# The sums of squares of the pre-norms by four column groups of 32, in a two-layer hybrid decoder step

## The reference

```
def rms_norm(x, g):
    xf = x.astype(F32)
    y = xf * lax.rsqrt(jnp.mean(xf * xf, axis=-1, keepdims=True) + RMS_EPS)
    return (y * g.astype(F32)).astype(x.dtype)
...
mod = (jax.nn.silu(c) @ a_w + a_b).reshape(B, N_SUB, 3, D_MODEL)[:, :, :, None, :]
def modulate(y, i):
    return rms_norm(y, g_pre[i]) * (1.0 + mod[:, i, 1]) + mod[:, i, 0]
def residual(y, out, i, w):
    return y + w * mod[:, i, 2] * rms_norm(out, g_post[i])
x = residual(x, swiglu(modulate(x, 0), f_in[0], f_out[0]), 0, FFN_RES_WEIGHT)
```

## Time and profile before

| | |
|---|---|
| median of 3 runs | 1376.84 us (1375.82 to 1381.52) |
| the profiled execution | 1375.88 us, of which the span is 1374.1 us |
| TensorE matmul busy | 1334.4 us (97%) |
| VectorE busy | 684.0 us (50%) |
| ScalarE busy | 539.0 us (39%) |
| line 569, busy over six norms | 31.5 us, 96 records |
| line 569's share of the chain that ended last | 1.4% |

### The profile page before, as it was taken

The page is one execution under the profiler, slowest core; times in us unless marked ns, Lnnn a source line. Parts: engine busy times, 40 slices in busy tenths (PEclk is TensorE's granted clock), DMA queues, the critical chain, the costliest instruction groups (busy, mean ns, idle before and its releaser), DMA issues.

```text
span 1374.1 us, 23261 instructions
## 1 busy us (share of the span) xinstructions
PE 1334.4 (97%) x10138; PEld 1238.2 (90%) x10138; DVE 684.0 (50%) x735; ACT 539.0 (39%) x641; POOL 85.1 (6%) x103
## 2 busy tenths in 40 slices
PE   6999999999989999999999999999999989999997
PEld 3899999979969699999979999998898779999996
DVE  3433434367875644434463344434778573444443
ACT  4423333343445533333343233333343554333331
POOL 0000000000270000000000000000017100000000
PEclk8999999999999999999999999999999999999999
DMA  9975566465325643446375544655542463344531
GB/s 363 344 257 191 185 236 224 152 231 214 123 95 227 226 161 144 153 176 261 115 276 200 181 142 152 240 190 214 203 150 68 163 254 123 142 150 141 196 136 39
DMA packets 50372, 255.43 MB, mean 186 GB/s; under 512 B 7022, under 2 KB 12014, under 8 KB 30062
## 3 DMA queue, kind: packets, MB, share of 16 engines
q1 hardware_dynamic: 50110, 253.08, 50.8%
q0 software_dynamic: 176, 1.09, 0.2%
HBM read 249.26 MB, written 4.89 MB: 185 GB/s over the span
## 4 chain that ended last, share of the span: by engine, by line
PE 94%; DVE 2%; DMA 2%; ACT 1%; issue 1%; SPq 0%; DVEq 0%; ACTq 0%
PE PS L505 28%; PE PS L507 27%; PE PS L506 27%; PE PS L517 3%; PE PS L569 1%; DMA z<-in_ada 1%; PE PS L704 1%; PE PS L723 1%; DMA stage<-in_ada_w 1%; PE PS L924 1%; PE PS L746 0%; DVE raw L1644 0%; PE PS L669 0%; PE PS L577 0%; PE PS L851 0%
## 5 line engine op out<-in xcount | busy, mean ns | idle before, releaser
L505 PE MATMUL PS<-hmh,WHI 128*128 128x320 f32 x1856 | 578.2, 312 | 7.0 <-DVE hml L1347 6.6
L506 PE MATMUL PS<-hml,WHI 128*128 128x320 f32 x1856 | 572.6, 309 | 0.0
L507 PE MATMUL PS<-hmh,WLO 128*128 128x320 f32 x1856 | 572.5, 308 | 0.0
L1304 DVE TENSOR_TENSOR WLO<-raw,WHI 128x2048 fp32r<-128x2048 f32 (+1 forms) x148 | 365.6, 2470 | 408.7 <-ACT WHI L1012 408.7
L1012 ACT ACTIVATE WHI<-raw 128x2048 fp32r<-128x2048 f32 (+1 forms) x148 | 303.9, 2053 | 356.9 <-PE PS L507 353.0
L505 PEld LDWEIGHTS PS<-hmh,WHI 128*128 128x128 f32 x1856 | 349.4, 188 | 28.1 <-issue 26.4
L506 PEld LDWEIGHTS PS<-hml,WHI 128*128 128x128 f32 x1856 | 349.6, 188 | 0.3
L507 PEld LDWEIGHTS PS<-hmh,WLO 128*128 128x128 f32 x1856 | 349.3, 188 | 0.0
L505 PE MATMUL PS<-hhl,WHI 128*128 128x320 f32 x704 | 216.6, 308 | 0.0
L506 PE MATMUL PS<-hhl,WHI 128*128 128x320 f32 x704 | 216.5, 308 | 0.0
L507 PE MATMUL PS<-hhl,WLO 128*128 128x320 f32 x704 | 216.5, 308 | 0.0
(11 more groups left out here) (247 smaller groups left out, 815.7 us busy)
## 6 DMA issues: line engine op xcount, KB each, us to landing
raw<-in_w_in SPq DMA_DIRECT2D x88, 1024.0 KB, 4.8
raw<-in_w_out SPq DMA_DIRECT2D x32, 1408.0 KB, 5.9
stage<-in_ada_w SPq DMA_DIRECT2D x82, 512.0 KB, 7.7
ada<-in_ada_w SPq DMA_DIRECT2D x46, 512.0 KB, 5.9
raw<-in_m_in SPq DMA_DIRECT2D x20, 1024.0 KB, 4.7
raw<-in_m_out SPq DMA_DIRECT2D x8, 1024.0 KB, 4.8
z<-in_ada SPq DMA_DIRECT2D x3, 1024.0 KB, 13.7
big<-in_ada SPq DMA_DIRECT2D x2, 1024.0 KB, 19.8
```

Source lines behind the costliest of these rows:

```text
L505: mm(out, hi, rhi, start=first, stop=False)
L506: mm(out, hi, rlo, start=False, stop=False)
L507: return mm(out, lo, rhi, start=False, stop=last)
L1304: tt(WLO[:, slot, 0:width], raw[:, slot, 0:width], WHI[:, slot, 0:width].bitcast(F32), ALU.subtract).then_inc(s_lo[slot], 1)
```

## The change

The eight products take only the first 32 columns of the ones. Product k goes to the quarter k % 4 of the PSUM partitions, so a quarter holds the sum of two tiles (k and k + 4), repeated on its 32 partitions. ScalarE copies the bank to `rt` in SBUF (`quads`, a new semaphore pair `s_xg`, `s_xc`), and one more product with the full block of ones (`x_total`) adds the 128 partitions, which is 32 times the total; the scale of Ln becomes 1 / (32 D). In a gap, `x_total` stands on TensorE behind the first of the pieces that follow `x_stats`; where none follow (fifth gap) it stands behind the transposes. At the start it stands right behind the eight products.

```diff
                 for k in range(KT):
                     pe.wait_ge(s_sqx, KT * n + k + 1)
-                    last = mm(PS[:, 5, 0:T], ones, sq[:, k, :], start=(k == 0), stop=(k == KT - 1))
-                last.then_inc(s_xst, 1)
+                    j = k % 4
+                    last = mm(PS[32 * j:32 * j + 32, 5, 0:T], ones[:, 0:32], sq[:, k, :], start=(k < 4), stop=(k >= 4))
+                last.then_inc(s_xg, 1)
+
+            def x_total(n):
+
+                pe.wait_ge(s_xc, n + 1)
+                mm(PS[:, 5, 0:T], ones, rt[:], start=True, stop=True).then_inc(s_xst, 1)
...
                 if p is not None:
                     for i in range(5, 5 + BEHIND[n]):
                         partial(p + i)
+                        if i == 5:
+                            x_total(n + 1)
+                if n < 3 * DEPTH - 1 and not BEHIND[n]:
+                    x_total(n + 1)
...
             x_stats(0)
+            x_total(0)
...
+            def quads(n):
+
+                act.wait_ge(s_xg, n + 1)
+                a_(rt[:], PS[:, 5, 0:T], ACT.Copy).then_inc(s_xc, 1)
+
             def x_rms(n, chunk=None):
...
                 if chunk is not None:
                     ada_copy(chunk)
-                rms(5, rst[:], s_r, 1.0 / D, s_xst, n + 1)
+                quads(n)
+                rms(5, rst[:], s_r, 1.0 / (32 * D), s_xst, n + 1)
...
+            quads(0)
             hi_split(0, 0, W_IN)
             act.wait_ge(s_xst, 1)
-            a_(rt[:], PS[:, 5, 0:T], ACT.Ln, bias=EPS, scale=1.0 / D).then_inc(s_rt0, 1)
+            a_(rt[:], PS[:, 5, 0:T], ACT.Ln, bias=EPS, scale=1.0 / (32 * D)).then_inc(s_rt0, 1)
```

More of the change, by code:

```diff
@@ L293, in trunk @@
         s_xst = sem("s_xst")
+        s_xg = sem("s_xg")
+        s_xc = sem("s_xc")
         s_r = sem("s_r")
```

## The result

The changed kernel takes 1381.72 us (median of 14 runs, 1377.76 to 1387.82), the kernel before, run beside it, 1377.48 us (14 runs, 1374.46 to 1381.52). The ratio is 1.0038, 95% interval 1.0026 to 1.0050: +5.2 us, slower by less than 0.5% (the two medians alone are 4.2 us apart). Forecast were no measurable change and 1378.3 us, in a range of 1375.0 to 1382.9.

The account below looks back on a forecast made before the run. It took the gaps to be bound by a latency chain from the squares of x to the entry. Terms 0.75 + 0.05 + 0.13 + 0.75 - 0.18 = +1.5 us moved the median 1376.84 to 1378.3 us, range 1375.0 to 1382.9.

Parts of the forecast that it names:

- not side by side: Rival, all gaps: narrow groups still take 0.60 us each, copy and last product come on top; +6.1 us, 1382.9 us, chance 0.07.
- lower end, 1375.0: Whole kernel: bottom of the range; fifth-gap clock falling later or returning sooner gave -2.4 us or 1374.4, with run spread added.
- First and fourth gap (+0.75 each): Gaps 1 and 4: copy and last product start Ln 0.75 us later, and the delay passes undiminished to the entry.
- Second gap (+0.05): Gap 2: the entry waits for the third piece's DMA, so nearly all delay is hidden; +0.05 us, 0.75 without that cover.
- Third gap (+0.13): Gap 3: earlier transposes gain VectorE 0.37 us, but the root becomes the late one; +0.13 us, bounds -0.37 and +1.0.
- the estimate that I made by that rule: Gap 3: tiling-mode changes drain TensorE, 0.21 us for each change more; the gap would lose 0.4 us more.
- Fifth gap (-0.18): Gap 5: VectorE gains 0.37 us from earlier transposes; the root sets line 1388 at 1125.27 against 1125.45, -0.18 us.
- the earlier return or later fall: Gap 5: TensorE's clock may fall later or return sooner, up to 2.6 us less.
- The start (0): First norm: it shrinks and gains copy and product, but TensorE then waits for a DMA until 23.37 us; 0 us.
- TensorE's busy time was to fall by some us: Sign in the changed profile: TensorE's busy time falls by some us while the span does not.
- the clock falls: Rival, gaps: less TensorE work lowers its clock; one or two falls +4.1 or +6.7 us, chance 0.06; three or more 0.03.
- nearest row: Profile row 461 to 465, TensorE busy 2.52 of 4 us at clock 1.00, cited for expecting no fall in the first gap.

Follow-up runs that it names:

- narrow-only kernel: Changed kernel without copy and second product in any norm, so three quarters of each sum are left out: 1377.75 us, 0.9986 of the kernel before.
- its product moved: Changed kernel with the last product right behind the narrow ones, ahead of transposes and pieces: 1379.49 us, 1.0013; with the wide start too, 1378.97 us, 1.0010.
- shifted kernel before: Kernel before with three useless products behind the start, some 1.6 us of TensorE work: 1380.97 us, 1.0030; the changed kernel shifted alike: 1382.81 us, 1.0048.
- two kernels with fill: Kernel before with useless products: six in the fifth gap, 1377.64 us, 0.9993; or three and four at the start and six there, 1379.91 us, 1.0012.

## Why the prediction was right, and where it was off

In the gaps the change did what was forecast: two chains of latencies grow by three quarters of a microsecond each and the rest nearly cancels. That the time lies in the range is in part luck. The range's upper end, 1382.9 us, came from the rival "not side by side", which did not happen, while most of the distance from the point comes from terms that were not in the sum at all. Its lower end, 1375.0, does not follow from its own terms, which gave 1374.4; nothing hung on that.

**First and fourth gap (+0.75 each): right**, +0.78 and +0.77. Each step came as written: the copy 0.82 us behind the last square (0.90 assumed), copy 0.44, last product 0.81, TensorE covering the copy with a piece. That a narrow product alone takes as long as a wide one was the assumption that decided this term, and it nearly holds: its reader starts 0.82 us behind the square, in the narrow-only kernel too, against 0.90 us with a wide one. The 0.08 us do not show in the sum, since the piece ends after the copy.

**Second gap (+0.05): within what a DMA decides.** It came out at +0.30, because the third piece waited for its data for 1.81 us, 1.48 before:

```profile
468.48 1.07 PE L519 MATMUL PS<-stage,cT 128*32 128x512 f32 x8 [1.81 <-DMA stage<-in_ada_w]
```

In the other profiles of kernels with the changed gap it takes 14.92 to 15.51 us, in those with the old one, leaving the one with a late transfer of 18.14 aside, 15.13 to 16.63. The transfer sets it, not the norm.

**Third gap (+0.13): mis-sized**, +0.42 (15.66 or 15.67 us in five of five profiles with this order and 15.23 to 15.25 in those of before). The steps that were mis-sized are durations on TensorE: Ln came 3.13 us behind the last square, 2.84 in the sum. By the starts of the records (the durations that the timeline prints hold a tail), the transposes began 0.70 us behind the square (0.65 in the sum), the piece 0.59 us behind them (0.45) and the last product 0.99 us behind the piece (0.89). At each of the three steps TensorE changes between 32 and 128 columns. What a change costs can be read where the last product of the norm meets the first transpose. The kernel before, the one with wide products copied and added, and the changed one:

```profile
708.65 0.43 PE L569 MATMUL PS<-sq,cst 128*128 128x320 f32 x1
708.92 0.27 PE L525 MATMUL PS<-cst,adp 128*128 128x128 f32 x1
```

```profile
712.49 0.43 PE L571 MATMUL PS<-sq,cst 128*128 128x320 f32 x1
712.75 0.27 PE L527 MATMUL PS<-cst,adp 128*128 128x128 f32 x1
```

```profile
712.08 0.43 PE L572 MATMUL PS<-sq,cst 128*32 128x320 f32 x1
712.44 0.33 PE L527 MATMUL PS<-cst,adp 128*128 128x128 f32 x1
```

The transpose starts 0.27 us behind the product where both are 128 columns wide, and 0.36 us where the product has 32: 0.09 us for the change, between two kernels that at this place differ in nothing else (the second and third). Three changes come to 0.28 us, and Ln was 0.29 us late, though step by step the lateness is less even (0.05, 0.14 and 0.10 us). The prediction saw no sign of this in the trace of before, since it added up totals of a chain of waits; the starts have it there too: from the last records of a piece to the first wide product 0.52 us, from piece to piece 0.43. The Trainium skill, "TensorEngine Tiling (Array Packing)", Key Properties, has a drain at such a change. The trace agrees, with 0.09 us for each; the estimate that I made by that rule, 0.21 us for each of two more changes (+0.53 in all), was nearer the measured +0.42 than my sum (+0.13).

**Fifth gap (-0.18): right in sign and mechanism**, -0.29: `mod_out` starts as soon as `lo_split` ends, and the root is no longer last. The clock is low there for 6.8 us in both, so the earlier return or later fall that widened the range did not come.

**The start (0): right by itself, open in the whole.** In the kernel before, and in the changed kernel with its product moved, the narrow norm there costs nothing; in the changed kernel the wide norm gives 3.2 us back.

**TensorE's busy time was to fall by some us:** 7.1 us are gone from the norm's lines, and 1.3 from the total. The clock can account for much of it: at the lower level work counts longer, and the level was low for 10.2 us more in this profile (13.7 against 10.2 us at the start, 6.8 in the first mixer), an estimate of up to 5 us.

**What the sum left out** is all that lies outside the gaps. I had taken a kernel whose other instructions are untouched to run as before there. Two things contradict it.

*Issue stops in the mixers.* In the second mixer they add 0.6 us, at the same two places and of the same length in both profiles of the changed kernel (1.19 and 0.88 us, then 1.19 and 0.90):

```profile
1058.21 0.69 PE L735 MATMUL PS<-sq 64*64 64x64 f32 x32 [1.19 <-issue]
```

```profile
1067.46 0.71 PE L787 MATMUL PS<-sq 64*128 64x128 f32 x8 [0.90 <-issue]
```

while the kernel before has 0.72 at the first of them and none at the second:

```profile
1051.68 0.57 PE L723 MATMUL PS<-sq 64*64 64x64 f32 x22 [0.72 <-issue]
```

From the first record of line 663 in it to the next gap this mixer takes 109.70 us before and 109.68 in the shifted kernel before; 110.34, 110.37 and 110.24 in the three profiles with the whole change.

What these stops are can be read from all 14 profiles together. The stop at line 663 (1.01 us) stands at the same line in every kernel. All others in the mixers but one of 0.19 us, 78 of 0.18 to 1.70 us, stand at seven places when TensorE's MATMUL records are counted from the first one: ahead of record 2626, 2752, 2879 and 3005 in the first mixer and 7690, 7816 and 8068 in the second (the first record is 0). These numbers are the same in kernels whose programs differ ahead of them by up to 16 records. They are 126 or 127 records apart, or twice that, which with the weight loads and waits between them is 255 to 258 TensorE records. And every one of the 78 ends 1.2 to 1.6 us after a packet of 16 KB has landed on queue 8, which the profile calls a queue of instructions. So TensorE stops at fixed numbers of instructions, just after the next block of them has come. An edit ahead moves the program against these boundaries, and that is how instructions that nobody touched get another duration. The lengths are not fixed by the program: ahead of record 2752 the changed kernel stops for 0.80 us in one profile and 1.35 in the other, and its first mixer has 3.2 and 4.6 us of stops in all. The shifted kernel before has 5.3 us there, with the clock at 1.00, and its first mixer takes 149.12 us against 146.40: a first mixer can be 2.7 us longer by stops alone.

*The mean clock.* It is 0.0016 lower in the changed kernel, in both of its sets, which at 1.05 us for 0.001 is 1.7 us. In the profiled execution it is the 3.2 us of the first mixer. The rival "the clock falls" had put this in the gaps and priced a fall at 2.6 us; price and nearest row held (in gaps one to four the clock stayed at 1.00 in every profile, but for the second gap of the two kernels with fill, where a transfer came late), the place was wrong. Falls come in the mixers: in 9 of the 14 profiles, 3.4 to 20.5 us in all, in kernels of every kind, but not in that of before, which was the only one that I could read.

The account of the measured +5.2 us (or +3.9 by the means of the table): +2.0 in the gaps and +0.6 in the second mixer are read from the profiles, as are 0.5 us more of stops in the first (1.9 in the kernel's second profile); +1.7 goes with the lower clock, an estimate from the slope over the runs, which can hold a part of the stops too; what is left lies within the errors. The latencies and the issue stops are shown. **Open** is why the clock is lower in the changed kernel. It is not the start's norm alone (start narrow in the kernel before: 0.9916), not the gaps alone (start wide in the changed kernel: 0.9918), and not when the kernel reaches the mixers (shifted: unchanged). Nor is it the narrow start together with the changed gaps as such: with the second product moved both are there, and the clock is 0.9911. One conjecture would be that issue stops leave TensorE idle in a mixer that is thin already and so bring the clock down. The profiles speak against it: the first mixer of the changed kernel fell with 3.2 and 4.6 us of stops, but in five profiles of other kernels it kept a clock of 1.00 with 3.4, 3.6, 3.8, 4.1 and 5.3 us.

## What to carry to other kernels

Before narrowing a reduction's products, ask what ends last: here the squares arrived one by one, the reader came only 1.64 us behind the last of them, and a copy and one more product are a longer way than the queue they remove. When a sum is made stage by stage from a trace, keep in its range what no edit touches but every edit moves: issue stops in unrolled stretches and the level of the clock in thin ones came to more here than the change's own cost. And time kernels that differ by 0.3% in two sets before explaining the difference, and don't read a fall of the clock in one profile as the work of the edit: undoing the start's part of the change gave nearly all of it back, the same part alone did nothing, and falls came in kernels of every kind, ahead of the edit too.

## What the runs showed of the hardware

- A lone fp32 product of 320 tokens takes nearly as long with 32 columns as with 128: its reader starts 0.81 to 0.82 us after the square in every kernel with narrow products, and 0.90 us after it with a wide one. What four side by side save is the queue: seven MATMUL records in 1.34 us, each of 0.43 us or more.
- A change between 32 and 128 stationary columns costs TensorE 0.09 us: 0.36 us instead of 0.27 from the last record of the norm to the first transpose, with the same instructions around it.
- TensorE stops for 0.2 to 1.7 us in unrolled stretches of small products, for nothing that the trace names, at the same seven MATMUL record numbers in all 14 profiles, about 256 TensorE records apart. The transfers of the second mixer of before include ten packets of a queue that moves instructions,

```profile
q8 instruction: 10, 0.16, 0.6%
```

  about 16 KB each, and each of the 78 stops ends 1.2 to 1.6 us after one of them has landed. That these stops are TensorE running out of instructions is a reading of these two facts; no run changed the blocks to test it.
- Useless products raised the clock where they stood (fifth gap, -2.1 us), as "TensorE: Matmul & The Clock Gate" of the Trainium skill, Part 1, would have it, where activity releases the throttle. But equally busy stretches of TensorE just ahead (6.27 of 6.80 us in both kernels) were followed by a fall in one kernel and none in the other, and fills at three places gained nothing over the whole kernel. How busy TensorE was in front of a place was not enough to predict the clock there.
